# Decoder layer with expert retrieval: query weights reloaded per chunk, their memory given to the row rings

## The reference, cut to what matters

```python
def chunk(xc):                      # 128 tokens
    qh = einsum('cd,de->ce', xc, wq)            # wq: 1024 x 1024, the query weights
    s1, s2 = scores of qh's halves against sub-keys k1, k2
    experts, top_s = best 16 of the 16 x 16 sums, in each of 8 heads
    gates = softmax(top_s)
    act = gelu(einsum('chkd,cd->chk', u_tab[experts], xc))
    return einsum('chk,chkd->cd', gates * act, v_tab[experts])
y = h + peer(rms_norm(h))
```

## Time and profile before

| | |
|---|---|
| median of three runs | 3090.54 us |
| the profiled execution, its span | 3482.5 us |
| share of the span: PE, DVE, POOL, ACT | 80%, 62%, 57%, 25% |
| moved by DMA in the span | 1121.47 MB, mean 322 GB/s |
| of this by POOL's gathers | 1073.87 MB |

### The profile page before, as it was taken

One profiled execution on the slowest core, in us unless ns is written; L12 is line 12 of the kernel. 1 busy time (PEld: TensorE's weight loads), 2 busy tenths in 40 slices (PEclk: granted clock), 3 DMA queues, 4 the chain that ended last, 5 costly groups with the idle time before them and its releaser, 6 DMA issues.

```text
span 3482.5 us, 30095 instructions
## 1 busy us (share of the span) xinstructions
PE 2791.4 (80%) x7609; PEld 1257.9 (36%) x7609; DVE 2152.2 (62%) x5205; ACT 875.1 (25%) x2053; POOL 1999.2 (57%) x2062
## 2 busy tenths in 40 slices
PE   8999488677887888687977888789877988677777
PEld 4445234233432334233432434234432444222222
DVE  1245966865677657756587567856676646744443
ACT  2331221123212331134112421135212532111111
POOL 1000466666666666666667556666666666766665
PEclk9999699999999999999999899999999999999999
DMA  6111799999999999999999889989999998999998
GB/s 216 33 31 67 262 361 343 347 363 370 346 347 352 373 350 328 357 358 364 344 359 357 326 335 331 362 339 342 359 339 358 338 350 321 348 377 359 369 356 343
DMA packets 320463, 1121.47 MB, mean 322 GB/s; under 512 B 36465, under 2 KB 44681, under 8 KB 320296
## 3 DMA queue, kind: packets, MB, share of 16 engines
q0 software_dynamic: 294912, 1073.87, 82.6%
q1 hardware_dynamic: 25384, 45.72, 3.8%
HBM read 1111.01 MB, written 8.45 MB: 321 GB/s over the span
## 4 chain that ended last, share of the span: by engine, by line
PE 24%; issue 20%; DVE 16%; another core or an unknown queue 10%; DMA 9%; POOL 8%; ACT 3%; POOLq 0%; DVEq 0%; ACTq 0%; SPq 0%
PE psum L1433 16%; DVE ring_u L1744 6%; DMA ring_v<-in_peer_v,experts 5%; POOL ring_v L1334 5%; DMA ring_u<-in_peer_u,experts 4%; POOL ring_u L1334 3%; PE psum L949 2%; PE psum L970 1%; PE psum L1391 1%; PE psum L1365 1%; PE psum L1381 1%; DVE acc L1700 1%; DVE top_i L1081 1%; DVE relu_z L1084 1%
## 5 line engine op out<-in xcount | busy, mean ns | idle before, releaser
L1433 PE MATMUL psum<-ring_v,diag 128*128 128x512 f32 x4076 | 2031.7, 628 | 454.2 <-DMA ring_v<-in_peer_v,experts 305.3
L1744 DVE CUSTOM_DVE_ANT_0 ring_u<-ring_u,psum 128x1024 f32<-128x1024 f32 x1024 | 1237.6, 1219 | 564.5 <-DMA ring_u<-in_peer_u,experts 469.9
L1334 POOL DMA_INDIRECT ring_u<-in_peer_u,experts x1024 | 990.9, 968 | 893.9 <-issue 623.3
L1334 POOL DMA_INDIRECT ring_v<-in_peer_v,experts x1024 | 997.5, 974 | 577.4 <-issue 279.1
L1433 PEld LDWEIGHTS psum<-ring_v,diag 128*128 128x128 f32 x4076 | 744.2, 198 | 1498.2 <-issue 1372.2
L1577 ACT ACTIVATE diag<-ident,weights 128x128 f32<-128x128 f32 x1019 | 360.1, 392 | 966.8 <-issue 348.3
L483 PE MATMUL psum<-w_sb,xnT 128*128 128x512 f32 x560 | 246.6, 599 | 0.0
L1700 DVE SCALAR_TENSOR_TENSOR acc<-conv_in,taps,acc 128x128 f32<-128x128 f32 x840 | 239.5, 348 | 9.4 <-remote 8.6
L1669 DVE TENSOR_TENSOR_SCAN log_keep<-log_keep,relu_z 128x256 f32<-128x256 f32 (+3 forms) x88 | 90.5, 1028 | 173.2 <-ACT log_keep L1510 86.9
L970 PEld LDWEIGHTS psum<-actT,w_kept 128*128 128x128 f32 x1024 | 136.8, 199 | 75.1 <-issue 75.1
L970 PE MATMUL psum<-actT,w_kept 128*128 128x128 f32 x1024 | 139.4, 282 | 21.3 <-issue 21.1
(11 more groups left out here) (188 smaller groups left out, 1570.5 us busy)
## 6 DMA issues: line engine op xcount, KB each, us to landing
ring_u<-in_peer_u,experts POOLq DMA_INDIRECT x1024
ring_v<-in_peer_v,experts POOLq DMA_INDIRECT x1024
w_sb<-in_w_in SPq DMA_DIRECT2D x4, 2048.0 KB, 19.6
x_in<-in_x SPq DMA_DIRECT2D x8, 512.0 KB, 4.4
w_kept<-in_w_out SPq DMA_DIRECT2D x1, 4096.0 KB, 13.6
h_res<-in_x SPq DMA_DIRECT2D x8, 512.0 KB
w_kept<-in_peer_wq SPq DMA_DIRECT2D x1, 4096.0 KB, 14.1
wo_sb<-in_w_out SPq DMA_DIRECT2D x1, 4096.0 KB, 12.7
```

The source lines that it names most:

```text
L1334: nc.gpsimd.indirect_dma_start(ring[kind][:, at, :], None, peer_u[0] if kind == "u" else peer_v[0], bass.IndirectOffsetOnAxis(S.experts[c ...
L1433: last = nc.tensor.matmul(y_ps[:, j * BANK:(j + 1) * BANK], diag[:, e % DIAGS, :], ring["v"][:, n % RING["v"], j * BANK:(j + 1) * BANK], s ...
L1744: nc.vector.tensor_tensor_reduce(out=row, in0=row, in1=hn, scale=1.0, scalar=0.0, op0=ALU.mult, op1=ALU.add, accum_out=dots[:, e:e + 1]).t ...
```

## The change

`w_kept` holds the query weights for chunk 0 alone; afterwards its 32 KB are eight row slots. With 12 new slots of 4 KB (as many as the two rings had) there are 20, 10 for u and 10 for v. For each of the fronts 1 to 7, SP loads the query weights anew: eight loads of 512 KB, four per half of the columns, into `relu_z[0]`, `relu_z[1]`, `attT` and `log_keep[0]`. The first four wait until the attention of this front has finished with the buffer, the second four until the queries of the first half have read it. `query` walks the blocks of the contraction outside and four heads inside, and waits for each buffer. SP's loads of q and the convolution's input keep their order and stand ahead of the weights.

```diff
--- before.py
+++ after.py
@@ -39,7 +39,8 @@
 EPS = 1e-6
 NEG = -1.0e30
 LOWEST = -3.0e38
-RING = {"u": 5, "v": 7}
+RING = {"u": 10, "v": 10}
+WQ_BUFS = 4
 LAG = 20
 SLOTS = ROWS
 DIAGS = 8
@@ -218,6 +219,10 @@
     S.o_T = nc.alloc_semaphore("o_T")
     S.o_copied = nc.alloc_semaphore("o_copied")
     S.wq_loaded = nc.alloc_semaphore("wq_loaded")
+    S.wq_in = [nc.alloc_semaphore(f"wq_in{n}") for n in range(WQ_BUFS)]
+    S.wq_read = nc.alloc_semaphore("wq_read")
+    S.wq_bufs = [b.rearrange("p (k n) -> p k n", n=BANK) for b in
+                 (relu_z[0][:, :], relu_z[1][:, :], attT[:, :, :].rearrange("p b t -> p (b t)"), log_keep[0][:, :])]
     S.g_loaded = nc.alloc_semaphore("g_loaded")
     S.x_in = nc.alloc_semaphore("x_in")
     S.mixed = nc.alloc_semaphore("mixed")
@@ -266,7 +271,7 @@
            conv_ln_b, w_out, norm_ffn_g, peer_wq, peer_k1, peer_k2)
     phase1(nc, S, late.at, psum, ident, ident_b, mask, kT, vals, keys_bd, w_kept, wo_sb, actT, qT,
            conv_in, acc, iota16, taps, g_attn, b_conv, g_ln, b_ln, qT_spill, hT_spill, x,
-           w_out, peer_u, peer_v, out)
+           w_out, peer_wq, peer_u, peer_v, out)
 
 
 def phase0(nc, S, base, psum, ident, ident_b, mask, kT, vals, keys_bd, w_kept, wo_sb, actT, qT,
@@ -963,14 +968,26 @@
         if n == 0:
             pe.wait_ge(S.h_copied, 2 * (f + 1))
             pe.wait_ge(S.h_done, f + 1)
-            pe.wait_ge(S.wq_loaded, 16)
+            if not later(f):
+                pe.wait_ge(S.wq_loaded, 16)
+        heads = PH // 2
         total = PH * KT_D
         for m in range(total * n // QUERY_SLOTS, total * (n + 1) // QUERY_SLOTS):
-            h, k = m // KT_D, m % KT_D
-            product = nc.tensor.matmul(z[0][:, h * P:(h + 1) * P], wq_sb[:, k, h * P:(h + 1) * P],
-                                       S.actT[:, k, :], start=k == 0, stop=k == KT_D - 1)
+            half, k, h = m // (heads * KT_D), m // heads % KT_D, m % heads
+            buf, kept = k // 2, k % 2
+            if later(f):
+                if kept == 0 and h == 0:
+                    pe.wait_ge(S.wq_in[buf], 16 * (2 * (f - 1) + half + 1))
+                weight = S.wq_bufs[buf][:, kept, h * P:(h + 1) * P]
+            else:
+                weight = wq_sb[:, k, (half * heads + h) * P:(half * heads + h + 1) * P]
+            product = nc.tensor.matmul(z[0][:, (half * heads + h) * P:(half * heads + h + 1) * P], weight,
+                                       S.actT[:, k, :], start=k == 0 and h == 0,
+                                       stop=k == KT_D - 1 and h == heads - 1)
             if m in (total // 2 - 1, total - 1):
                 product.then_inc(S.queried, 1)
+            elif later(f) and half == 0 and kept == 1 and h == heads - 1:
+                product.then_inc(S.wq_read, 1)
 
     def score_keys(f, pair):
 
@@ -1209,9 +1226,11 @@
 
 def phase1(nc, S, base, psum, ident, ident_b, mask, kT, vals, keys_bd, w_kept, wo_sb, actT, qT,
            conv_in, acc, iota16, taps, g_attn, b_conv, g_ln, b_ln, qT_spill, hT_spill, x,
-           w_out, peer_u, peer_v, out):
+           w_out, peer_wq, peer_u, peer_v, out):
     m = Map(nc, base)
-    ring = {kind: m.tile(f"ring_{kind}", [P, RING[kind], D], F32) for kind in "uv"}
+    fresh = m.tile("ring", [P, RING["u"] + RING["v"] - KT_D, D], F32)
+    slots = [fresh[:, n, :] for n in range(RING["u"] + RING["v"] - KT_D)] + [w_kept[:, n, :] for n in range(KT_D)]
+    ring = {"u": slots[:RING["u"]], "v": slots[RING["u"]:]}
     diag = m.tile("diag", [P, DIAGS, P], F32)
     small = Map(nc, m.at)
     bn = small.tile("bn", [P, 6], F32)
@@ -1284,24 +1303,50 @@
         @block.sync
         def _(sp):
             def load_front(f):
-                if later(f):
-                    sp.wait_ge(S.z_ready, UNITS * f)
-                    sp.dma_start(qT[:, :, :].rearrange("p b t -> p (b t)"),
-                                 qT_spill[f]).then_inc(S.q_in, 16)
-                    sp.wait_ge(S.tapped, TAP_OPS * f)
-                    sp.dma_start(conv_in[:, :, :], hT_spill[:, :, f * P:f * P + HALO + P]).then_inc(S.c_in, 16)
-                    sp.wait_ge(y_begun, f)
-                    sp.dma_start(S.h_res[:, :], x[0, f * P:(f + 1) * P, :]).then_inc(S.x_in, 16)
+                sp.wait_ge(S.z_ready, UNITS * f)
+                sp.dma_start(qT[:, :, :].rearrange("p b t -> p (b t)"),
+                             qT_spill[f]).then_inc(S.q_in, 16)
+                sp.wait_ge(S.tapped, TAP_OPS * f)
+                sp.dma_start(conv_in[:, :, :], hT_spill[:, :, f * P:f * P + HALO + P]).then_inc(S.c_in, 16)
+
+            def load_x(f):
+                sp.wait_ge(y_begun, f)
+                sp.dma_start(S.h_res[:, :], x[0, f * P:(f + 1) * P, :]).then_inc(S.x_in, 16)
+
+            def load_query_weights(f):
+
+                for half in range(2):
+                    for b in range(WQ_BUFS):
+                        if half and b == WQ_BUFS - 1:
+                            sp.wait_ge(S.queried, 2 * f + 1)
+                        elif half:
+                            sp.wait_ge(S.wq_read, (WQ_BUFS - 1) * (f - 1) + b + 1)
+                        elif b < 2:
+                            sp.wait_ge(S.att_T, UNITS * (f + 1))
+                        elif b == 2:
+                            sp.wait_ge(S.attended, HEADS * (f + 1))
+                        else:
+                            sp.wait_ge(S.o_T, f + 1)
+                        sp.dma_start(S.wq_bufs[b],
+                                     peer_wq[0, 2 * b * P:2 * (b + 1) * P, half * BANK:(half + 1) * BANK]
+                                     .rearrange("(k p) n -> p k n", p=P)).then_inc(S.wq_in[b], 16)
 
             def store(c):
                 sp.wait_ge(y_copied, c + 1)
                 sp.dma_start(out[0, c * P:(c + 1) * P, :], y_out[:, :]).then_inc(y_stored, 16)
 
             def step(c, f):
+                if c is None:
+                    load_front(1)
+                    return
                 if f is not None:
-                    load_front(f)
-                if c is not None and later(c):
+                    load_x(f)
+                if later(c):
                     store(c - 1)
+                if f is not None:
+                    if f + 1 < CHUNKS:
+                        load_front(f + 1)
+                    load_query_weights(f)
 
             over_chunks(step)
             store(CHUNKS - 1)
@@ -1332,7 +1377,7 @@
                     hold(pool, row_added, pe_rows(before), pool_passed)
                 at = n % RING[kind]
                 nc.gpsimd.indirect_dma_start(
-                    ring[kind][:, at, :], None, peer_u[0] if kind == "u" else peer_v[0],
+                    ring[kind][at], None, peer_u[0] if kind == "u" else peer_v[0],
                     bass.IndirectOffsetOnAxis(S.experts[c % 2][:, e:e + 1], 0)).then_inc(row_in[kind][at], 16)
 
             def tail():
@@ -1344,7 +1389,7 @@
 
         @block.tensor
         def _(pe):
-            mix, transpose_h, query, score_keys = tensor_front(nc, pe, S, (z_ps, w_ps), wo_sb, w_kept)
+            mix, transpose_h, query, score_keys = tensor_front(nc, pe, S, (z_ps, w_ps), wo_sb, None)
 
             def scores(f, a, u):
 
@@ -1431,7 +1476,7 @@
                 is_last = e == ROWS - 1 or c == CHUNKS - 1 and e == ROWS - 2
                 for j in range(2):
                     last = nc.tensor.matmul(y_ps[:, j * BANK:(j + 1) * BANK], diag[:, e % DIAGS, :],
-                                            ring["v"][:, n % RING["v"], j * BANK:(j + 1) * BANK], start=False,
+                                            ring["v"][n % RING["v"]][:, j * BANK:(j + 1) * BANK], start=False,
                                             stop=is_last)
                 last.then_inc(row_added, 1)
 
@@ -1740,7 +1785,7 @@
                     dve.wait_ge(gelued, PH * (c - 1) + e // TOPK + 1)
                 n = row_of(c, e)
                 dve.wait_ge(*landed("u", n))
-                row = ring["u"][:, n % RING["u"], :]
+                row = ring["u"][n % RING["u"]]
                 nc.vector.tensor_tensor_reduce(out=row, in0=row, in1=hn,
                                                scale=1.0, scalar=0.0, op0=ALU.mult, op1=ALU.add,
                                                accum_out=dots[:, e:e + 1]).then_inc(dotted, 1)
@@ -1758,7 +1803,7 @@
             def add_row_aside(n, e):
 
                 at = row_of(CHUNKS - 1, e)
-                row = ring["v"][:, at % RING["v"], :]
+                row = ring["v"][at % RING["v"]]
                 dve.wait_ge(*landed("v", at))
                 if n == 0:
                     dve.wait_ge(y_stored, 16 * (CHUNKS - 1))
```

## The result

The changed kernel takes 3147.05 us (median of four runs, 3145.96 to 3148.19) against 3090.14 us for the kernel before: a ratio of 1.0184, 95% interval 1.0172 to 1.0196. It is slower by 57 us; 3141 was forecast, inside 3098 to 3180.

The account below looks back on a forecast made before the run. The prediction took the DMA engines, at a ceiling of 412 GB/s, to bound the kernel. From 3090.5 us it added 76 for reloading weights and subtracted 25 for deeper rings, other terms 0: 3141 us, range 3098 to 3180.

Parts of the forecast that it names:

- the 392 us: Whole kernel before: its profiled span, 3482.5 us, exceeds the median of 3090.54 by 392 us, with the same bytes.
- The reload: Seven fronts load weights again, 29.4 MB in 2 KB pieces at 387 GB/s: 76 us, on the path in full.
- The rings: Gather stage: ten slots each for u and v return DMA time left idle by a full ring, 25 us.
- The 15 us at the start stay mostly: First 55 us of the gather stage: 15 us of DMA idle time, mostly not returned by the larger rings.
- the 43 us: Gather stage after its start: 58 - 15 = 43 us of DMA idle, of which 25 was taken as returned.
- PE's waits for the weights: In `query`, PE waits for each weight buffer; loads were expected to land in time, so 0 us.
- the stalls with empty rings: Gather stage: POOL stalls though slots are free, as before a v gather after 5.16 us idle; expected to remain.
- the split of the idling into two kinds: POOL's stalls before gathers: one kind with slots free (5.16 us), one for want of a u slot (0.81 us).
- The faster one: Gather stage: POOL and the u ring hold the runs, rings return 100 us; 2991 or 3029 us, chance 0.08.
- The no-change one: Gather stage: rings return all idle, 74 us, and weights cost 71 to 76; 3088 to 3093 us, chance 0.06.
- The slower one by PE's wait: Second half of `query`: loads later than 18 us stop PE; 3176 us, 3211 with no cover, chance 0.12.
- The case that the rings return nothing: Gather stage: all idling has slots free, so 3166 us; inside the prediction's own case, 3100 to 3167, chance 0.74.

Follow-up runs that it names:

- second profile of before: The kernel before, unaltered, profiled again on a chip where its runs take 3090 us: span 3089.3 us, ratio 1.0001.

## Why the prediction was right, and where not

**The bound.** That the DMA engines are the ceiling was right, and more so than written: in the second profile of before they are all but full from 420 us on. The reading of the 392 us was wrong. I took them for the profile's own cost (under "how the profile stands to the runs"); a kept trace costs nothing, and the same loss shows in every run on chip 1. The conclusion drawn, that most of the idling in that trace is not in the runs, held all the same, because it was made from the median and the bytes, not from the trace's shares.

**The reload**, 76 us from 387 GB/s: 76.7 and 76.3 measured. That it lies on the path in full: shown by half the bytes costing half.

**The rings**, 25 us: 17.6 and 17.2 measured. The size is nearly half again too large and the place was wrong. "The 15 us at the start stay mostly" is the step that failed: the start gave 11 to 12 us, and of the 43 us that I put elsewhere 7 came, in one chunk. The 43 came of dividing the stage's bytes by 407 and 412 GB/s, the rates of stretches of 10 and 20 us; over 2360 us the full engines move 404, and 1088 MB at 404 take 2693 us of the 2714, which leaves 21. The two errors run against each other, 11 to 12 us too little at the start and 18 too much in the middle, so that the term came out only 8 us off is in part luck. It explains the miss: 3090.1 + 76.5 - 17.4 = 3149, where 3141 was forecast and 3147 to 3149 measured.

**PE's waits for the weights**, 0: right. 9 to 11 us to landing against 18, and no wait on DMA at L984.

**The profile's signs.** Bytes up by 29 MB, no waits in `query`, fewer u gathers held by dots (156 times in the second profile of before, at most 124 after), a mean rate of 403 GB/s where 404 was said ((1088 + 29) / 2770): right. A DMA share above 0.94 with GB/s up holds only against the trace shown of before; against its second profile nothing moved (1.02 and 404 before, 1.02 and 405 after, from 700 to 3060 us), so this sign told nothing of the change. A span of 3440 to 3600 and the stalls with empty rings still there: wrong, both being of the slow kind, which the changed kernel's profile is not of. For the same reason the stall at 3243 us, on which the split of the idling into two kinds rested, says nothing of the runs of 3090 us.

**The rivals.** The faster one needed over 413 GB/s on average, and there is none: a chip without the stalls moves 403 to 406. The no-change one needed the rings to return 74 us. The slower one by PE's wait needed over 18 us to landing, and the loads took 9 to 11. The case that the rings return nothing has its 3166 us in the kernel with the small rings. The Trainium skill's 425 GB/s (DMA: Bandwidth & Descriptors, section Bandwidth, Measured), for one 16 MB load, is not reached by rows of 4 KB here; its 408.7 for a stream of loads from SP in 4 KB rows (the same page, section on iDMA) agrees with 403 to 409 in full stretches.

## What to carry to other kernels

Before memory is bought with extra transfers, ask what share of the run the DMA engines are already full: here 29.4 MB cost 2.6 us per MB with nothing hidden, while eight more slots returned 17 us, two thirds of it once, at the start. Where the engines are full, a deeper ring makes the queue longer and not the rate higher; moving one slot from the ring that seldom holds POOL up to the one that often does gave 5 us at no cost, and a second one lost it again. To place a gain of some us, compare when the same row is reached in both traces, not the rates of fixed stretches. And where a profile's span is far from the median of the runs, take a second profile before the idle time in it is counted as idle time of the kernel.

## What was not expected of the hardware

The same kernel takes 3090 us on one chip and 3469 on another, with runs that lie within 7 us (3086 to 3093) and 29 us (3451 to 3480) of each other. Only one chip was seen in the slow kind, in one set of runs, so whether it is the chip or what else went on there at the time isn't settled. There the DMA engines run at 0.95 and 357 GB/s even with ten slots each and no reload, and extra bytes cost nothing that shows. The stretch of 420 to 3380 us there, with the small rings and the reload:

```profile
420.00:3380.00 2960.00, 2349.04 (x6357) 1044.47 (x6355) 1923.31 (x4573) 741.84 (x1776) 1919.19 (x1963) 0.95 0.96 362
```

And with the large rings and no reload:

```profile
420.00:3380.00 2960.00, 2349.08 (x6435) 1086.95 (x6433) 1929.62 (x4616) 746.74 (x1799) 1956.41 (x1994) 0.92 0.95 357
```

With it go stops of POOL's queue. `hold` leaves a record (L93) for each slot that POOL is let into. In the trace shown of before, the view of that line ahead of the stall of the earlier trace rows, 3210 to 3233 us:

```profile
L93 POOLq EVENT_SEMAPHORE  x19: 17/17/17, 3210.0 to 3232.6; - x19
```

And inside it, 3233.3 to 3242.3 us:

```profile
nothing on L93; most used: ['L1433', 'L1744', 'L1334', 'L1430']
```

19 in 23 us, and then none in 9 us, though the slots needed had come free. In the waits a v gather stands up to 5.0 us for a PE row there, and in the second profile of before at most 1.6. Two more things set the slow traces apart. With ten slots and no reload the gathers hold the DMA engines for 83.8% of 3419.6 us, 2866 us, where 88.3% of 3071.2 us, 2712 us, do on the fast kind, for the same 1073.87 MB; so the packets themselves take 6% longer, and the stops are not the whole loss. And each of the five slow pages puts 8 to 13% of its chain to `another core or an unknown queue`, none of the nine fast ones any. From the page of the trace shown of before:

```profile
PE 24%; issue 20%; DVE 16%; another core or an unknown queue 10%; DMA 9%; POOL 8%; ACT 3%; POOLq 0%; DVEq 0%; ACTq 0%; SPq 0%
```

What stops the queue, and why there alone, was not found and not tried.
